# A state-space recurrence on one core: the order of weighing, splits, evacuation and logarithm in three engines' streams

## The reference, cut to what matters

```
xbc = silu(causal_dwconv(xbc, conv_w, conv_b)); xs, bm, cm = split(xbc)
dt  = softplus(dt_raw + dt_bias);  a = -exp(a_log);  X = xs * dt
cb  = C . B per group;  y = (cb * exp(segsum(dt * a))) . X, + the earlier chunks' states
y   = (y + xs * d_skip) * silu(z)
y   = y * rsqrt(mean(y * y over the group's 256) + EPS) * norm_g
```

## Time and profile before

| | |
|---|---|
| median of 3 runs | 1767.96 us (1767.52 to 1768.05) |
| profiled execution | 1767.69 us |
| its span, first to last instruction | 1766.0 us |
| mean granted clock of TensorE | 0.997 |
| TensorE busy | 1737.2 us (98%) |
| VectorE busy | 1205.4 us (68%) |
| ScalarE busy | 751.6 us (43%) |

### The profile page before, as it was taken

How to read it: one execution, slowest core, us unless ns; L and a number is a source line. 1 busy time by engine, 2 the same in 40 slices (tenths; PEclk the granted TensorE clock), 3 DMA queues, 4 the chain that set the end, 5 groups by cost and what they waited for, 6 DMA issues and landing times.

```text
span 1766.0 us, 34047 instructions
## 1 busy us (share of the span) xinstructions
PE 1737.2 (98%) x13394; PEld 1658.9 (94%) x13394; DVE 1205.4 (68%) x1705; ACT 751.6 (43%) x1043; POOL 8.2 (0%) x35
## 2 busy tenths in 40 slices
PE   7999999999999999999999999999999999999997
PEld 7999899999999999999999899999989999999886
DVE  7788766556467778784335778788885788878333
ACT  5445532134243232322223777777874323223222
POOL 0000000000000000000000000000000000000000
PEclk9999999999999999999999999999999999999999
DMA  4322332222222323232223222222212322323221
GB/s 148 109 96 85 96 109 72 72 72 61 73 93 84 95 83 95 83 104 97 84 85 102 64 75 76 75 75 76 84 61 86 94 90 88 95 89 102 99 97 65
DMA packets 42557, 154.17 MB, mean 87 GB/s; under 512 B 4960, under 2 KB 5984, under 8 KB 41840
## 3 DMA queue, kind: packets, MB, share of 16 engines
q1 hardware_dynamic: 41296, 146.49, 26.4%
q10 hardware_dynamic: 1184, 6.60, 1.1%
HBM read 146.62 MB, written 2.13 MB: 84 GB/s over the span
## 4 chain that ended last, share of the span: by engine, by line
PE 79%; DVE 10%; issue 7%; ACT 4%; DVEq 0%; POOL 0%; ACTq 0%; POOLq 0%
PE gp L420 72%; DVE wlo L1220 2%; DVE lb L1752 1%; PE small L532 1%; PE small L456 1%; DVE xcv L1260 1%; PE small L611 1%; PE small L673 1%; DVE dec L1343 1%; DVE sp_lo L1710 1%; ACT lbuf L1063 1%; ACT lbuf L1061 1%; ACT whi L771 1%; ACT L1066 0%; ACT lbuf L1066 0%
## 5 line engine op out<-in xcount | busy, mean ns | idle before, releaser
L420 PE MATMUL gp<-hn_hi,whi 128*128 128x264 f32 (+1 forms) x3200 | 659.7, 287 | 6.8 <-DVE vr L1250 2.6
L420 PE MATMUL gp<-hn_hi,wlo 128*128 128x264 f32 (+1 forms) x3200 | 650.0, 285 | 0.0
L420 PE MATMUL gp<-hn_lo,whi 128*128 128x264 f32 (+1 forms) x3200 | 649.3, 284 | 0.0
L771 ACT ACTIVATE whi<-raw 128x1024 fp32r<-128x1024 f32 (+1 forms) x249 | 273.9, 1100 | 740.7 <-PE gp L420 739.2
L1220 DVE TENSOR_TENSOR wlo<-raw,whi 128x1024 fp32r<-128x1024 f32 (+1 forms) x249 | 317.4, 1275 | 316.4 <-ACT whi L771 316.2
L420 PEld LDWEIGHTS gp<-hn_hi,whi 128*128 128x128 f32 x3200 | 500.4, 189 | 12.5 <-DVE wlo L1220 4.7
L420 PEld LDWEIGHTS gp<-hn_lo,whi 128*128 128x128 f32 x3200 | 496.5, 189 | 0.0
L420 PEld LDWEIGHTS gp<-hn_hi,wlo 128*128 128x128 f32 x3200 | 496.0, 189 | 0.0
L420 PE MATMUL gp<-hid_hi,whi 128*128 128x264 f32 (+1 forms) x528 | 140.9, 321 | 0.0
L420 PE MATMUL gp<-hid_hi,wlo 128*128 128x264 f32 (+1 forms) x528 | 140.9, 321 | 0.0
L420 PE MATMUL gp<-hid_lo,whi 128*128 128x264 f32 (+1 forms) x528 | 140.8, 321 | 0.0
(11 more groups left out here) (249 smaller groups left out, 1744.4 us busy)
## 6 DMA issues: line engine op xcount, KB each, us to landing
raw<-in SPq DMA_DIRECT2D x217, 512.0 KB, 3.5
raw<-in SPq DMA_DIRECT2D x32, 704.0 KB, 4.0
cs_bc<-cs_scratch ACTq DMA_DIRECT2D x4, 1056.0 KB, 5.9
hT<-in SPq DMA_DIRECT2D x4, 528.0 KB, 7.7
q_turned<-qs SPq DMA_DIRECT2D x16, 132.0 KB, 4.2
k_turned<-ks SPq DMA_DIRECT2D x16, 132.0 KB, 4.1
out<-yT SPq DMA_DIRECT2D x8, 256.0 KB, 2.4
rdec<-in ACTq DMA_DIRECT2D x1, 1056.0 KB, 6.5
```

What stands on the lines that cost most here:

```text
L420: ins = pe.matmul(psum[:, h, 0:width], wp[w.par][:, cols], rp[:, k0 + k, q0:q0 + width], start=first and k == 0 and n == 0, stop=last and ...
L771: act.activation(whi[w.par][:, 0:kt * P], raw[w.par][:, 0:kt * P], ACT.Copy).then_inc(hi_done, 1)
```

## The change

Four edits of order; no instruction is added or taken away.

- VectorE, slot 4: the second pair's decays are weighed ahead of the low split, not behind it.
- VectorE, slot 5: low split and evacuation of the first z tile come ahead of the second pair's output (take(g, 1)); before, the order was output, split, sum of the squares, evacuation.
- ScalarE, first unit of a stage (and units 0 and 6 of retention's first eight): the high split comes ahead of the logarithm (step 6), not between logarithm and exponential (step 7).
- TensorE: the sum over the partitions is put into its unit behind k tile 3, not behind k tile 1.

```diff
@@ TensorE @@
             def ssd_back(g):
-                return lambda k: ssd_sums(g) if k == 1 else None
+                return lambda k: ssd_sums(g) if k == 3 else None
@@ ScalarE, ssd_stage @@
                     if c == 0:
                         ssd_small(g - 1, 0)
+                    split_hi(At(6, g, W_SSD + c + 1))
                     if back:
                         ssd_small(g - 2, 6)
-                    split_hi(At(6, g, W_SSD + c + 1))
-                    if back:
                         ssd_small(g - 2, 7)
@@ ScalarE, retention's first eight units @@
+                split_hi(At(8, 0, W_RET + c + 1))
                 if c in back:
                     ssd_small(back[c], 6)
-                split_hi(At(8, 0, W_RET + c + 1))
-                if c in back:
                     ssd_small(back[c], 7)
@@ VectorE, ssd_slot @@
                 elif c == 4:
+                    weigh_pair(g, 1)
                     split_lo(w)
-                    weigh_pair(g, 1)
                     tile(3)
                     take(g, 0)
                     conv_(3)
                 elif c == 5:
+                    split_lo(w)
+                    tile(4)
                     take(g, 1)
-                    split_lo(w)
                     add_pair(g)
-                    tile(4)
```

## The result

The changed kernel takes 1773.19 us (median of 8 runs, 1772.01 to 1774.10) against 1767.76 us (8 runs, 1767.34 to 1768.28): ratio 1.0030, 95% interval 1.0021 to 1.0039. It is slower by 5.4 us; 4.7 were forecast.

A forecast was written before the change was run, and what follows sets the result against it. A VectorE-ScalarE loop of 47.26 us per stage was taken as longer than TensorE's; three times 1.87, plus 1.06 and 0.1 us, put the third transposes at 209.21 against 204.51: +4.7 us, 1772.7 us, range 1769.5 to 1774.8.

The forecast's parts named there:

- Weighing ahead of the split costs nothing: VectorE, slot 4: decays 1.25 us sooner, split ends 3.1 us later with its readers not held up; cost nothing.
- part 1: VectorE's weighing ahead of the low split: cost nothing, gain up to 0.2 and 0.7 us at L500's two waits.
- 1.87 us more in each pass, carried: VectorE, slot 5: output starts 1.25 + 0.62 us later; the VectorE-ScalarE loop accumulates 1.87, 3.74, 5.61 us.
- The transposes: TensorE, L448, waiting for the logarithm: starts at 110.58, 160.09 and 209.21 us, late by 0.3, 2.9 and 4.7 us.
- The slack read from rows 6 and 7: From the logarithm's end on ScalarE to TensorE's transposes in the old profile: 2.0 us, 2.1 one stage on, 2.7 one before.
- The sum of 4.7 us: Total slowdown: third pass's transposes at 209.21 instead of 204.51 us; nothing after 255 us gives time back.
- The stops: TensorE idle ahead of the transposes: about 3.1 us in the second pass, about 2.9 us in the third.
- the rival: TensorE's clock falls in the new stops; behind the third it costs its full 1.5 us: 1774.2 us, chance 0.31.
- The third logarithm decides alone: TensorE catches up between logarithms, but the next takes it back; only the last one's 4.7 us delay counts.
- The later sum is free: TensorE's sum of squares two k tiles later: no cost; left at k == 1 it would cost up to 0.5 us.
- ScalarE's split ahead of the logarithm: ScalarE's 1.06 us high split goes first: its readers see no change, the logarithm ends 1.87 + 1.06 = 2.93 us later.

The follow-up runs named there:

- filling the idle time: In VectorE's slot 1, first tile's evacuation and x times dt moved ahead of the low split: kernel before 1765.83 us (0.9991), changed kernel 1769.86 us (1.0011).

## Why the prediction was right

Direction, size and mechanism held; how the 4.7 us were shared out among the edits held only in part. By its own steps, with the changed kernel's times moved by the 0.48 us by which its first products (94.42 instead of 94.90) were early:

- *Weighing ahead of the split costs nothing.* Right within the noise: decays are ready, the weights are not late (alone +0.3 us, inside its interval). The gain of up to 0.9 us, which part 1 took, is no gain in time: the waits go and come back at the next unit. The sum did not rest on it.
- *1.87 us more in each pass, carried.* Right: the outputs start at 100.44, 149.84 and 199.09 on before's scale, against 98.55, 146.17 and 193.43 before with 1.87, 3.74 and 5.61 added: 100.42, 149.91 and 199.04. The run with this edit alone shows the same periods, and filling the idle time takes 2.2 of the 5.7 us back at the third output.
- *The transposes.* Forecast 110.58, 160.09, 209.21; measured 110.53, 159.93, 209.18. The first wait, of 0.3 us, stands in no list of waits, but the transposes there start 0.47 us after the start of the last matmuls instead of 0.24. The slack read from rows 6 and 7 was the right one: the logarithm alone, 1.06 us later, was free.
- *The sum of 4.7 us.* The middle has 4.8. The run times have 5.4, 0.7 more than forecast; the profile's other parts are -0.5 and +1.2 us in start and tail, outside the changed code, and add up to that. The forecast had no term for them, and whether they belong to the change or came by luck one profile of each can't tell.
- *The stops.* 3.1 and 2.9 us were forecast, 2.92 and 1.89 measured. The second is shorter because the clock fell behind the first, as the rival had it: from the transposes to the next first-pair products TensorE took 23.1 us (159.45 to 182.55) instead of 21.5 (157.18 to 178.72). That ate 1.6 us, the 0.3 us left at L500 and most of the rest out of the next stop. The third logarithm decides alone, so this cost nothing. A fall behind the third stop, which the rival priced at 1.5 us, did not come; nothing in the prediction decides it, and that much was luck. The rival leaned on one fall behind a stop of 1.53 us; nine of the twelve profiles have the same stop without a fall.
- *The later sum is free.* Right in the changed kernel, since ScalarE gets to its logarithm only at 157.16; wrong as a general statement, since with VectorE's old order and the logarithm late it costs about 1 us (0.9 by the medians, 1.6 by the middles). At k == 1 I gave its wait for acc at most 0.5 us; it was 1.23 and 1.18 us. That cost nothing either, as the transposes behind it wait for the logarithm.
- *ScalarE's split ahead of the logarithm.* I had it at 1.06 us of the 4.7, so that undoing it would give 1.1 us back. It gives nothing back: the transposes start earlier, but the weights of the next unit are then 0.8 to 0.9 us late. Without this edit the unit's start would have been the same within 0.1 us (210.0 against 210.1 and, in the changed kernel, 209.74 + 0.48 = 210.2). My sum was right because it followed the path that decides in the changed kernel; its split into 3.6 us for the output and 1.1 for the logarithm was not, and that the second path ends so close to the first I had not seen.

## What to carry to other kernels

A wait of the busiest engine on a helper engine can be the visible end of a loop between two helpers; then moving work ahead of a link of that loop costs that work once per pass, and the waits that the move removes come back elsewhere. Find the place where one helper stands idle for the other, and put independent work there: here one moved line gave 1.9 us by the median, with an interval that just reaches no change, and 1.3 by the middle. Follow a late instruction to every counter that it raises, also to those that only protect a bank or a buffer.

## What the runs showed of the hardware

TensorE's granted clock fell to its lower level behind the one stop of 2.92 us (0.93 and 0.73 in the windows of 5 us from 155 and 160 us), behind one of 1.86 us (0.77 and 0.89), and behind two of 1.96 and 0.91 us that lie 1 us apart (0.50 and 0.81). It did not fall behind stops of 1.89 and 1.36 us, nor behind the four of 1.2 to 1.5. Near 40 us, ahead of the changed code, every one of the twelve profiles has a stop of 1.5 us at the same matmul: behind it the clock fell in three (the kernel before, the changed kernel with the logarithm ahead again, and the logarithm late only: 0.73, 0.64 and 0.53 from 40 to 42 us) and stayed at 1.00 in nine. So stops of the same length fall on either side, and the length alone doesn't decide; what does, no run here shows. The page "TensorE: Matmul & The Clock Gate" of the Trainium skill (section "Why this matters for your kernels") asks for no idle gaps above about 3 us between bursts of matmuls. The fall behind 2.92 us lies at that figure; those behind 1.86 and 1.5 us came at shorter gaps.

The same clock goes with the length of this kernel's tail, where TensorE has only a few small products between waits. Where eight of the last small matmuls take 1.16 or 1.17 us, the tail takes 10.8 us (four profiles of twelve); where they take 2.07 or 2.08, 11.6 to 12.0 (three). The kernel before and the changed kernel (their timelines):

```profile
1756.82 1.17 PE L759 MATMUL small<-cst,frs 128*128 128x128 f32 x8 [0.57 <-DVE frs L1844]
```

```profile
1761.46 2.08 PE L759 MATMUL small<-cst,frs 128*128 128x128 f32 x8 [0.56 <-DVE frs L1842]
```
